# Attention scores of two heads at a time on the two halves of TensorE's rows, in a hybrid gated-MLP and sparse-attention block

## The reference

```python
def block(args):                       # one block of 128 queries
    ...                                # idx_score: indexer, relu(logits) summed over 8 heads
    _, sel = lax.top_k(idx_score, topk)            # 256 keys of those admissible
    valid = (sel // CHUNK) <= qchunk[None, :, None]
    k_sel, v_sel = gather(k, sel), gather(v, sel)
    scores = jnp.einsum('bqhd,bqkd->bhqk', qb, k_sel).astype(jnp.float32) * scale
    dist = jnp.abs(qpos[None, :, None] - sel).astype(jnp.float32)
    scores = scores - slopes[None, :, None, None] * dist[:, None]
    scores = jnp.where(valid[:, None], scores, NEG)
    p = jax.nn.softmax(scores, axis=-1).astype(v.dtype)
    return jnp.einsum('bhqk,bqkd->bqhd', p, v_sel)
```

## Time and profile before

| | |
|---|---|
| median of 3 timed runs | 568.47 us |
| profiled execution | 568.53 us |
| its span | 566.7 us |
| TensorE busy | 546.9 us, 97% |
| VectorE busy | 442.4 us, 78% |
| ScalarE busy | 371.4 us, 66% |
| granted TensorE clock, mean | 0.999 |

### The profile page before, as it was taken

One profiled execution on the slowest core, in us unless ns is written; L12 is line 12 of the kernel. 1 busy time (PEld: TensorE's weight loads), 2 busy tenths in 40 slices (PEclk: granted clock), 3 DMA queues, 4 the chain that ended last, 5 costly groups with the idle time before them and its releaser, 6 DMA issues.

```text
span 566.7 us, 8941 instructions
## 1 busy us (share of the span) xinstructions
PE 546.9 (97%) x2974; PEld 463.5 (82%) x2974; DVE 442.4 (78%) x1105; ACT 371.4 (66%) x711; POOL 185.3 (33%) x287
## 2 busy tenths in 40 slices
PE   8999999999999999999999998989999999999997
PEld 8997788878888888887888886778788888888886
DVE  4775778899979998999879867787787788767631
ACT  5885767767997667878987558655555565646520
POOL 1760000014449996676220004741212031201130
PEclk9999999999999999999999999999999999999999
DMA  8623110013231111221112237111202111020122
GB/s 251 217 61 107 57 38 20 1 38 94 92 93 39 40 53 38 58 74 45 54 54 74 84 122 223 57 56 57 85 27 64 49 42 54 20 75 0 38 75 75
DMA packets 39982, 39.69 MB, mean 70 GB/s; under 512 B 6144, under 2 KB 28160, under 8 KB 39936
## 3 DMA queue, kind: packets, MB, share of 16 engines
q1 hardware_dynamic: 38416, 39.11, 22.9%
q10 hardware_dynamic: 1520, 0.01, 0.1%
HBM read 30.72 MB, written 8.39 MB: 69 GB/s over the span
## 4 chain that ended last, share of the span: by engine, by line
PE 75%; DVE 14%; ACT 5%; issue 3%; DMA 1%; POOL 1%; SPq 0%; ACTq 0%; DVEq 0%
PE ps_proj L1068 37%; PE ps_proj L1232 11%; PE ps_proj L1204 5%; PE ps_tp L1189 5%; PE ps_lg L1095 4%; PE ps_lg L1096 4%; PE ps_lg L1232 3%; DVE cand L1470 2%; DVE w_lo L1377 2%; DVE score L1423 1%; PE ps_tp L1153 1%; DVE xT_lo L1691 1%; PE ps_tp L1085 1%; DMA kvi_raw<-in_w_in_dram 1%; PE ps_tp L1225 1%
## 5 line engine op out<-in xcount | busy, mean ns | idle before, releaser
L1068 PE MATMUL ps_proj<-w_hi,xT_hi 128*128 128x512 f32 (+1 forms) x432 | 164.4, 381 | 1.3 <-DVE w_lo L1377 0.9
L1068 PE MATMUL ps_proj<-w_lo,xT_hi 128*128 128x512 f32 (+1 forms) x432 | 161.1, 373 | 0.0
L1068 PE MATMUL ps_proj<-w_hi,xT_lo 128*128 128x512 f32 (+1 forms) x432 | 161.1, 373 | 0.0
L911 ACT ACTIVATE ps_lg<-score,cand 128x768 f32<-128x768 f32 (+2 forms) x96 | 96.1, 1001 | 10.3 <-DVE cand L1470 10.3
L1068 PEld LDWEIGHTS ps_proj<-w_hi,xT_hi 128*128 128x128 f32 x432 | 81.4, 188 | 15.1 <-DVE w_lo L1377 2.1
L1068 PEld LDWEIGHTS ps_proj<-w_lo,xT_hi 128*128 128x128 f32 x432 | 81.4, 188 | 14.8
L1068 PEld LDWEIGHTS ps_proj<-w_hi,xT_lo 128*128 128x128 f32 x432 | 81.5, 189 | 12.2
L968 ACT CAST xT_hi<-ps_tp 128x512 fp32r<-128x512 f32 (+3 forms) x96 | 43.8, 483 | 57.7 <-PE ps_tp L1189 57.6
L1691 DVE TENSOR_TENSOR xT_lo<-ps_tp,xT_hi 128x512 fp32r<-128x512 f32 (+3 forms) x96 | 50.8, 553 | 31.2 <-ACT xT_hi L968 31.0
L1377 DVE SCALAR_TENSOR_TENSOR w_lo<-stage,g_in,w_hi 128x512 fp32r<-128x512 f32 x48 | 43.1, 906 | 10.0 <-ACT w_hi L771 9.2
L952 ACT ACTIVATE lo_f<-lo_f,negmax 128x128 f32<-128x128 f32 (+7 forms) x64 | 50.3, 785 | 0.2
(11 more groups left out here) (177 smaller groups left out, 1105.7 us busy)
## 6 DMA issues: line engine op xcount, KB each, us to landing
stage<-in_w_in_dram SPq DMA_DIRECT2D x48, 256.0 KB, 2.7
x_in<-in_x_dram SPq DMA_DIRECT2D x8, 512.0 KB, 4.8
lo_f<-in_x_dram SPq DMA_DIRECT2D x7, 512.0 KB, 4.0
out_dram<-lo_f SPq DMA_DIRECT2D x7, 512.0 KB, 3.5
q_scratch<-nat SPq DMA_DIRECT2D x8, 256.0 KB, 2.1
q_in<-q_scratch SPq DMA_DIRECT2D x8, 256.0 KB, 3.8
stage<-in_w_out_dram SPq DMA_DIRECT2D x8, 256.0 KB, 2.7
z_scratch<-nat SPq DMA_DIRECT2D x8, 256.0 KB, 2.0
```

Of the source, the lines that this page charges most:

```text
L911: act.activation(ps_lg[i % 2][:, 0:keys(t)], score[:, sc_off[t]:sc_off[t] + keys(t)], ACT.Sign, bias=cand[:, t:t + 1].bitcast(F32), scale= ...
L1068: mm = pe.matmul(ps_proj[u % 2][:, 0:n], a[:, k, rows], b[:, k, 0:n], start=(k == 0 and i == 0), stop=(k == KB - 1 and i == 2))
```

## The change

`q_stack` is laid out by pairs of heads: the even head in rows 0 to 63 and the odd head in rows 64 to 127, hi parts of the four pairs first, lo parts behind. A product now takes 64 rows: rows 0 to 63 for the even head, writing ps_lg0, rows 64 to 127 for the odd head, writing ps_lg1. A pair and bank of keys has three of them for each head, hi·hi, lo·hi and hi·lo, even and odd in turn; lo·lo is left out. Scores of a pair are issued together, on even heads, ahead of that head's `pT`; they wait for both banks, and each bank has a semaphore of its own. `hi_q` and `lo_q` become one instruction each on 128 rows.

```diff
@@ tp_release(key)
             if kind == "q":
-                return q_lo_done, 2 * key[1] + 2
+                return q_lo_done, key[1] + 1
@@ ScalarE
             def hi_q(t):
                 if t >= 2:
-                    act.wait_ge(s_done, H * (t - 1))
+                    for odd in range(2):
+                        act.wait_ge(s_done[odd], H // 2 * (t - 1))
                 act.wait_ge(qT_done, t + 1)
-                for odd in range(2):
-                    half = slice(HALF * odd, HALF * (odd + 1))
-                    act.activation(q_stack[t % 2][0:HALF, odd:H:2, :],
-                                   ps_tp[tp_slot[("q", t)]][half, :].rearrange("p (h s) -> p h s", h=H // 2),
-                                   ACT.Copy, scale=gq[half, 0:1]).then_inc(q_hi_done, 1)
+                act.activation(q_stack[t % 2][:, 0:H // 2, :],
+                               ps_tp[tp_slot[("q", t)]][:, :].rearrange("p (h s) -> p h s", h=H // 2),
+                               ACT.Copy, scale=gq[:, 0:1]).then_inc(q_hi_done, 1)
@@ TensorE
             def scores(t, h):
                 m = head_no(t, h)
-                if h < 2:
-                    pe.wait_ge(q_lo_done, 2 * t + h + 1)
+                if h == 0:
+                    pe.wait_ge(q_lo_done, t + 1)
                 if m >= 2:
-                    pe.wait_ge(max_done, m - 1)
-                dot_keys(ps_lg[m % 2], q_stack[t % 2], h, k_hh, k_ll, keys(t)).then_inc(s_done, 1)
+                    pe.wait_ge(max_done, m)
+                j = h // 2
+                terms = ((j, k_hh), (H // 2 + j, k_hh), (j, k_ll))
+                for a in range(0, keys(t), BANK):
+                    b = min(keys(t), a + BANK)
+                    for i, (part, key) in enumerate(terms):
+                        for odd in range(2):
+                            half = slice(HALF * odd, HALF * (odd + 1))
+                            mm = pe.matmul(ps_lg[odd][:, a:b], q_stack[t % 2][half, part, :], key[half, a:b],
+                                           start=(i == 0), stop=(i == 2))
+                            if b == keys(t) and i == 2:
+                                mm.then_inc(s_done[odd], 1)
...
             scores(0, 0)
-            scores(0, 1)
...
                     if m % 2 == 0 and m > 0:
                         pv(m // 2 - 1)
+                    if m % 2 == 0 and m + 2 < T * H:
+                        scores(*divmod(m + 2, H))
                     pT(t, h)
-                    if m + 2 < T * H:
-                        scores(*divmod(m + 2, H))
@@ VectorE
             def lo_q(t):
-                for odd in range(2):
-                    dve.wait_ge(q_hi_done, 2 * t + odd + 1)
-                    ...
+                dve.wait_ge(q_hi_done, t + 1)
+                dve.scalar_tensor_tensor(
+                    out=q_stack[t % 2][:, H // 2:H, :],
+                    in0=ps_tp[tp_slot[("q", t)]][:, :].rearrange("p (h s) -> p h s", h=H // 2),
+                    scalar=gq[:, 0:1], in1=q_stack[t % 2][:, 0:H // 2, :].bitcast(F32),
+                    op0=ALU.mult, op1=ALU.subtract).then_inc(q_lo_done, 1)
...
             def bias_max(t, h):
                 m = head_no(t, h)
-                dve.wait_ge(s_done, m + 1)
+                dve.wait_ge(s_done[m % 2], m // 2 + 1)
```

More of the change, by code:

```diff
@@ L320, in hybrid_block @@
         q_lo_done = sem("q_lo_done")
-        s_done = sem("s_done")
+        s_done = [sem(f"s_done{i}") for i in range(2)]
         max_done = sem("max_done")
```

## The result

| | before | after |
|---|---|---|
| median, 4 timed runs each | 568.49 us | 584.11 us (584.09 to 584.37) |
| ratio to before, 95% interval | | 1.0276 [1.0264, 1.0288] |
| span of the profiled execution | 566.7 us | 582.1 us |
| TensorE waits from 317 us on, listed | 9.9 us | 19.0 us |

The change costs 15.6 us. The forecast was 6.0 us slower: the sign was right, the size was less than half of it. The granted TensorE clock was 0.999 in the profiled execution before and 1.000 in the one after, so the clock plays no part.

The account below looks back on a forecast made before the run. TensorE, busy 97% of the span, was taken to bound the kernel, also through the cover it gives others. 568.5 - 8.7 (slots) + 5.8 (switches) + 8.9 (lost cover) = 574.5 us; range 566 to 601.

Parts of the forecast that it names:

- a kernel without overlap: Rival: the array halves never work at once, six score products in a row in place of four; 600.6 us, chance 0.18.
- The likeliest case: Forecast case alone, halves overlapping, with switches and lost cover at their bounds: 568.7 up to 582.4 us, chance 0.45.
- Serial loads: Rival: halves overlap but their weight loads don't, so scores save only 2.5 us; 580.7 us, chance 0.15.
- Term 1: Scores on TensorE: three product slots a pair in place of four, 8.7 us less; at worst 17.4 more.
- Term 2: Switches between whole-array and half-array products, 64 at 0.09 us: 5.8 us more, bounds nothing to 10.2.
- Term 3: Scores leave the stretch behind even pT, TensorE waits in tiles 4 to 7: 8.9 us more, bounds 4.5 to 12.4.
- Terms 4 and 5: Scores' wait for both banks, covered by P·V; hi_q and lo_q as single instructions, off the path: nothing for each.
- The rival "faster": Halves overlap, switches cost nothing, chain to odd pT shortens by half of what it loses: 564.3 us, chance 0.16.

Follow-up runs that it names:

- the kernel with the heads in turn: Changed kernel with the six products of a pair and bank reordered, three of the even head, then three of the odd head: 584.81 us (ratio 1.0284).
- the order alone: Kernel before, its whole-array products issued for both heads of a pair on even heads, ahead of that head's pT: 583.21 us (ratio 1.0257).
- the last kernel: Kernel before with one output step moved from head 0 to 1 and one from head 4 to 5: 568.97 us against 568.59 (ratio 1.0007).

## Why the prediction was wrong in size

The measured 584.1 lies inside the range of 566 to 601, but by luck: the range reached that far for a kernel without overlap, and the overlap is there. The likeliest case, which has the mechanism right, was bounded by 582.4. Serial loads at 580.7 were nearer in number than the forecast of 574.5, but their mechanism isn't in the rows.

**Term 1, the overlap: right.** Slots of a pair stand 0.23 apart at 512 columns, three a bank. At 128 columns a block of six takes 0.48 (317.41 to 317.89 below), 0.20 of it the first load and the way out of term 2; the other 0.28 is less than three loads of 0.11 in a row, so the loads of the two halves overlap as well. Both rivals that denied this, at 580.7 and 600.6, fall, the second by the rows and by the kernel with the heads in turn. The Trainium skill (TensorEngine Tiling (Array Packing), Tiling Modes, Key Properties) has different tiles loading and multiplying in parallel; these rows agree. The Trainium skill (TensorE: Matmul & The Clock Gate, Part 3) had row groups together, some 4 ns apart (it gives no type of number for that figure); the changed kernel agrees with 3 to 4 ns. The pair of tile 0:

```profile
317.41 0.44 PE L1188 MATMUL ps_lg<-k_hh,xT_hi 64*128 64x128 f32 x4
317.69 0.28 PE L1188 MATMUL ps_lg<-k_ll,xT_hi 64*128 64x128 f32 x2
317.89 0.50 PE L1067 MATMUL ps_proj<-w_hi,xT_hi 128*128 128x512 f32 x1
```

**Term 2, the switches: too cheap.** I took 0.09 for each, the price of another kind of switch, and the trace has that 0.09 at both ends of the block; but the first load of a block, not made ahead, adds another 0.11: 0.29 a pair, 9.3 us for 32 where I had 5.8. The upper end that I had kept, 10.2, was nearer. The Trainium skill (TensorEngine Tiling (Array Packing), Tiling Modes, Key Properties) says that a change of mode drains the engine; the loads above agree with it, and the prediction had set the 10.2 beside it. The 0.09 that I called a switch of operand type is seen only behind transposes, and no run separates the type from the transposition; the other way round, from whole-array scores to transposes, nothing is added (0.23 above). By starts, from the first score to the transpose behind, and 0.09 for the way in, a pair now takes 0.58, 0.64, 0.82, 0.98, 1.26, 1.33, 1.51 and 1.67 us in tiles 0 to 7; four of each are 35.2 us against the 34.9 of before. Terms 1 and 2 together are +0.3, not -2.9. On the chip the same difference, the changed kernel less the one with whole-array products in the same order, is +0.9.

**Term 3, the lost cover: the step that failed.** It was right as a mechanism and mis-sized: 8.9 us forecast, 14.7 measured by the order alone, above even its upper bound of 12.4. I had also said that some 7.5 us of it would be idle time before pT in the odd heads; the listed waits there rose by 1.9, and the others stand before the transposes of q, y and the mixture and before P·V. By place, extra time from pT to pT with the scores' own time taken out, tiles 4 to 7:

| from head to head | forecast | measured | limit |
|---|---|---|---|
| 0 to 1 and 1 to 2 | 2.6 | 4.7 | sum over y; q's transposes |
| 2 to 3 | 1.9 | 1.85 | exponentials |
| 3 to 4 | 0.9 | 1.9 | lo_pT for P·V |
| 4 to 5 | 3.0 | 3.1 | lo_pT for y's transposes; sum over y |
| 5 to 6 | 0.5 | 1.0 | mixture's transposes |
| rest | 0 | 0.4 | |
| sum | 8.9 | 12.9 | |

Where I had read a chain instruction by instruction (2 to 3, 4 to 5) the forecast holds to 0.1, though at 4 to 5 some 2.2 of the 3.1 are waits before the transposes of y, and the waits for the sum over y there stayed as they were (0.79 before and 0.78 after in the last tile). What failed is the list of places. The q transposes at head 2 follow in an odd head's stretch as well, and I never asked what they wait for: of the 2.1 us missing in the first row all but 0.1 are in tiles 4 to 6, and tile 7 has no transposes of q. At head 3 to 4 I took 2.54 us from pT to the end of lo_pT, where P·V starts 2.66 after pT (539.07 - 536.41), and left out the restart behind a wait: from the first P·V product after its wait to the second 0.22 pass in place of 0.12. The P·V in question, last tile:

```profile
539.07 0.39 PE L1214 MATMUL ps_proj<-xT_hi,v_hl 128*128 128x256 f32 x1 [0.17 <-DVE xT_lo L1698]
```

The bound of 12.4 was itself made of tiles 4 to 7. Tiles 0 to 3, put at nothing, have 2.4 (0.2, 0.3, 0.4, 1.5): most of it in tile 3, where the 0.46 of scores of a head had been cover too. 12.9 + 2.4 + 0.3 = 15.6, where the two spans differ by 15.4: the sum is good to 0.2. Lost cover is thus 15.3 by this trace and 14.7 by the run with the order alone; to what the last 0.6 belongs is open.

**Terms 4 and 5, right at nothing.** No listed wait of the scores (L1188) on a maximum is there, so the wait for both banks is covered by P·V. The q instructions took 9.6 and 10.5 us and take 4.8 and 5.2, and no listed wait of TensorE is put down to them; no run changed them alone.

**The rival "faster"** said that VectorE and ScalarE, relieved, would shorten the chain by half of what it loses. From pT of head 4 to the second half of pT of head 5 it took 3.70, 3.93, 4.12 and 4.39 us in tiles 4 to 7 before and takes 3.70, 3.93, 4.13 and 4.39 after: it doesn't shorten. From head 0 to 1 it does, by 0.9 in the four tiles together, where half of what was lost would have been 4.5 in all.

What stays open: why half rows cost 0.9 in one place and 2.6 in the other. By tile it is above all in tile 3 (0.0 and 0.75); one candidate, not shown, is that ahead of pT a part of the switches falls into time in which TensorE waits anyway.

## What to carry to other kernels

When a change moves an engine's work from one stretch to another, list every instruction in both stretches that waits on another engine, also those that wait for nothing today: each has a slack, and the work removed in front is to be held against the smallest one. Filling one wait by moving work from another place is a gain only if that place has slack of its own; the last kernel gained nothing.

Packing two small products side by side saves slots but pays for each change of array form, so it is worth it only for long blocks (here between 512 and 640 columns a pair it began to save, at most 0.3 us a tile) and perhaps where all neighbours have the same form, which no run tried; measure the lone switch first, and never read the cost of lost cover from idle time alone where ends are modelled.

## What was not expected of the hardware

- Products on rows 0 to 63 and rows 64 to 127 do not start in program order between them. With three products of the even head ahead of the odd head's first, that first one still starts 10 ns after the even head's first, and the block takes 1.59 us (522.25 to 523.84) where it takes 1.58 with the heads in turn (521.73 to 523.31).
- A change of array form costs 0.175 us a switch in fp32r with one 128-column product between two of them, and the first weight load behind it begins only with its own product; in the kernel it is 0.29 us for the two switches of a pair.
- Two weight loads on different halves don't add up: at 128 columns, the six products of a pair take 0.28 us without the switches, where three whole-array ones take 0.33.
